# A two-layer decoder trunk in split fp32: layers written out, one weight slot merged, first low parts made on chip, one projection spread among the first logits

## The reference

```python
for l in range(DEPTH):                       # DEPTH = 2, S = 512, D = 1024, D_FF = 2816
    x = x + 0.5 * swiglu(rms_norm(x, ffn1_norm[l]), ffn1_gate[l], ffn1_up[l], ffn1_down[l])
    h = rms_norm(x, mix_norm[l])
    z = h @ w_in[l]
    aq, ak, av, iq, ik, iw, pu, mq = jnp.split(z, IN_OFFSETS, axis=-1)
    # aq, ak: 8 heads x 64, rms-normed; iq: 4 x 64; ik: 64; iw: 4; pu: 4 x 64; mq: 4 x 64
    y_attn = dsa_attention(aq, ak, av, iq, ik, iw)
    y_pool = multiscale_pool(pu, w_pool[l], pool_scale[l])
    y_mem = memory_attention(mq, rms_norm(mem, mem_norm[l]), w_mem_kv[l], ...)
    x = x + jnp.concatenate([y_attn, y_pool, y_mem], axis=-1) @ w_out[l]
    x = x + 0.5 * swiglu(rms_norm(x, ffn2_norm[l]), ffn2_gate[l], ffn2_up[l], ffn2_down[l])
```

## Time and profile before

| | us |
|---|---|
| median of 3 runs | 1970.55 |
| lowest, highest | 1969.13, 1972.46 |
| the profiled execution, its own time | 1967.57 |
| its span | 1965.5 |
| TensorE busy in it | 1918.9 |
| VectorE, ScalarE, GpSimd busy | 614.1, 1082.7, 347.6 |

### The profile page before, as it was taken

One profiled execution on the slowest core, in us unless ns is written; L12 is line 12 of the kernel. 1 busy time (PEld: TensorE's weight loads), 2 busy tenths in 40 slices (PEclk: granted clock), 3 DMA queues, 4 the chain that ended last, 5 costly groups with the idle time before them and its releaser, 6 DMA issues.

```text
span 1965.5 us, 27449 instructions
## 1 busy us (share of the span) xinstructions
PE 1918.9 (98%) x9148; PEld 1559.4 (79%) x9148; DVE 614.1 (31%) x1176; ACT 1082.7 (55%) x1391; POOL 347.6 (18%) x400
## 2 busy tenths in 40 slices
PE   6999999999899999999999999999998999999999
PEld 4888888887668888888878888888876688888887
DVE  3222210367662322220052222004677542222101
ACT  6655543565475755553375556336656566565432
POOL 1111111112511111111111111111125011111110
PEclk9999999999999999999999999999999999999999
DMA  8988888788236888888868888888781279888887
GB/s 219 215 190 191 194 193 193 184 197 193 76 87 150 199 197 191 192 193 192 194 162 201 191 193 189 199 192 199 177 205 48 70 173 221 192 193 193 194 190 184
DMA packets 97703, 354.07 MB, mean 180 GB/s; under 512 B 10976, under 2 KB 11232, under 8 KB 97376
## 3 DMA queue, kind: packets, MB, share of 16 engines
q0 software_dynamic: 47232, 171.99, 49.2%
q1 hardware_dynamic: 49824, 178.81, 27.7%
q10 hardware_dynamic: 576, 2.36, 0.3%
HBM read 179.05 MB, written 2.10 MB: 92 GB/s over the span
## 4 chain that ended last, share of the span: by engine, by line
PE 94%; DMA 2%; DVE 1%; issue 1%; ACT 1%; DVEq 0%; SPq 0%; ACTq 0%; POOLq 0%
PE bank L472 92%; PE bank L821 1%; DMA w_lo<-raw 1%; DMA raw<-weights 1%; ACT w_lo L932 0%; DMA x<-x_t 0%; DVE z L1315 0%; DVE mk_n L1321 0%; ACT prob L1086 0%; DVE t L1364 0%; ACT kv L1049 0%; ACT t L1086 0%; ACT w_hi L931 0%; DVE pt L344 0%; PE bank L744 0%
## 5 line engine op out<-in xcount | busy, mean ns | idle before, releaser
L931 ACT ACTIVATE w_hi<-raw 128x1024 fp32r<-128x1024 f32 x329 | 348.4, 1059 | 617.6 <-PE bank L472 592.1
L472 PE MATMUL bank<-h_hi,w_hi 128*128 128x512 f32 x1664 | 656.0, 394 | 15.6 <-ACT h_hi L903 13.6
L472 PE MATMUL bank<-h_hi,w_lo 128*128 128x512 f32 x1664 | 651.5, 392 | 5.7 <-DMA w_lo<-raw 5.7
L472 PE MATMUL bank<-h_lo,w_hi 128*128 128x512 f32 x1664 | 634.3, 390 | 0.0
L395 POOL DMA_DIRECT2D w_lo<-raw x328 | 282.6, 863 | 1556.5 <-ACT w_lo L932 1517.3
L472 PEld LDWEIGHTS bank<-h_hi,w_hi 128*128 128x128 f32 x1664 | 314.9, 189 | 88.5 <-ACT h_hi L903 15.1
L472 PEld LDWEIGHTS bank<-h_hi,w_lo 128*128 128x128 f32 x1664 | 314.7, 189 | 71.9 <-DMA w_lo<-raw 6.2
L472 PEld LDWEIGHTS bank<-h_lo,w_hi 128*128 128x128 f32 x1664 | 313.2, 188 | 66.2 <-issue 1.4
L932 ACT ACTIVATE w_lo<-raw 128x1024 fp32r<-128x1024 f32 x329 | 342.8, 1042 | 0.0
L472 PE MATMUL bank<-a_hi,w_hi 128*128 (+1 forms) x832 | 324.6, 390 | 0.0
L472 PE MATMUL bank<-a_lo,w_hi 128*128 (+1 forms) x832 | 323.8, 389 | 0.0
(11 more groups left out here) (143 smaller groups left out, 1226.2 us busy)
## 6 DMA issues: line engine op xcount, KB each, us to landing
raw<-weights SPq DMA_DIRECT2D x332, 512.0 KB, 4.7
w_lo<-raw POOLq DMA_DIRECT2D x328, 512.0 KB, 5.8
x<-x_t SPq DMA_DIRECT2D x4, 512.0 KB, 7.1
mem<-mem_t ACTq DMA_DIRECT2D x2, 1024.0 KB, 7.4
out_t<-x SPq DMA_DIRECT2D x8, 256.0 KB, 2.2
const<-consts SPq DMA_DIRECT2D x1, 481.5 KB, 10.0
wpool<-pool_w ACTq DMA_DIRECT2D x2, 128.0 KB, 7.2
par<-params SPq DMA_DIRECT2D x1, 38.0 KB, 1.8
```

The lines of the kernel that those rows point to most:

```text
L472: return nc.tensor.matmul(out_, lhsT, rhs, start=start, stop=stop, skip_group_check=True)
L931: nc.scalar.activation(w_hi[:, s], raw[:, s], ACT.Copy).then_inc(w_hi_done, 1)
```

## The change

- The two layers are written out on every engine instead of looped; the ring place of a slot is now `(l * SLOTS + n) % RING` (`place_of`), and the four dummy slots at the end of the stream are gone.
- ik and iw share one slot (64 columns and 4 columns); VectorE copies ik to both halves of `idx` in two operations. A layer has one slot fewer.
- In the indexer's section VectorE's work is reordered: the squares of the memory come after `cols`, the eight low parts of the memory (`m_lo`) after the scores; ScalarE rounds ik's successor after `idx_hi`.
- At the start SyncE issues slot 0 first. ScalarE writes its high part; VectorE writes its low part by subtraction, and both parts of slot 1; GpSimd both parts of slot 2. GpSimd also passes on that x has landed.
- At the start of the second layer `project_first` takes the order of the other thirds, and ScalarE rounds ahead at the end of the first layer as elsewhere.
- ScalarE loads the table with Silu before each ffn loop.
- In the tail mq 1 goes ahead of the spread, pu 0 and `heads_sum(2)` ahead of the transposes of `mk_n`. pu 1 goes in three pieces behind the logits of units 0, 2 and 4 (`RAMP`), into bank 5; VectorE evacuates it at unit 6. The first `pool_map` moves from unit 28 to 30.

```diff
-MIX_SLOTS = (("iq", 2), ("ik", 1), ("iw", 1), ("av", 4), ("aq", 4), ("ak", 4), ("kv", 4), ("mq", 2),
+MIX_SLOTS = (("iq", 2), ("ik", 1), ("av", 4), ("aq", 4), ("ak", 4), ("kv", 4), ("mq", 2),
...
-POOL_UNITS = (28, 32)
+POOL_UNITS = (30, 32)
+RAMP = {0: (4, 5, 6), 2: (7, 0, 1), 4: (2, 3)}
...
+            load(0, 0)
+            sp.dma_start(par[:, :], params[:, :]).then_inc(params_loaded, 16)
+            load_x(0)
+            load_x(1)
+            load(1, 1)
+            load_x(2)
+            load_x(3)
+            load(2, 2)
...
+                if pos < BEGUN:
+                    sp.wait_ge(first_lo[pos], 1)
...
+            pool.wait_ge(w_loaded[2], 16)
+            G.tensor_copy(w_hi[:, s], raw[:, s]).then_inc(first_hi[1], 1)
+            pool.wait_ge(first_hi[1], 1)
+            G.tensor_tensor(out=w_lo[:, s], in0=raw[:, s], in1=w_hi[:, s].bitcast(f32),
+                            op=ALU.subtract).then_inc(first_lo[2], 1)
...
-                if ph == 0:
-
-                    pe.wait_ge(w_hi_done, l * SLOTS + (n + 1))
+                if l == 0 and ph == 0:
+
+                    pe.wait_ge(w_hi_done, 1)
...
-                project(l, at("iw"), bank[3][:, :], h_hi, h_lo)
...
+                project_z(13, "mq", 1)
+
                 pe.wait_ge(spread_ready, l + 1)
...
-                project_z(13, "mq", 1)
-
-
+                project_z(14, "pu", 0)
+                heads_sum(2)
                 pe.wait_ge(mk_n_ready, l + 1)
...
-                project_z(14, "pu", 0)
-                heads_sum(2)
-                project_z(15, "pu", 1)
                 root_columns(2)
...
-                pe.wait_ge(proj_ready, (l + 1) * PROJ)
+                pe.wait_ge(proj_ready, (l + 1) * PROJ - 1)
...
+                    if n in RAMP:
+                        pool_part(RAMP[n])
...
-            with pe.Fori(0, LAYERS) as l:
+            for l in range(LAYERS):
...
+                nc.scalar.preload_act_table(ACT.Silu)
...
-                for n in range(rounds * RING, FC - 1 if e == 0 else FC - RING + 1):
+                for n in range(rounds * RING, FC - RING if l == LAYERS - 1 and e == 1 else FC - 1):
...
+                    if n == 6:
+                        evacuate(15, MIX_BASE["pu"] + 1, chunk(u, 1), bank[5][:, :], r[:, :])
...
+            V.tensor_tensor(out=w_lo[:, 0:SLOT], in0=raw[:, 0:SLOT], in1=w_hi[:, 0:SLOT].bitcast(f32),
+                            op=ALU.subtract).then_inc(first_lo[0], 1)
+            s = slice(SLOT, 2 * SLOT)
+            dve.wait_ge(w_loaded[1], 16)
+            V.tensor_copy(w_hi[:, s], raw[:, s]).then_inc(first_hi[0], 1)
...
```

More of the change, by code:

```diff
@@ L80 @@
 X_PARTS = 4
+BEGUN = RING - 1
 NEG = -1e30
@@ L321, in query_tile, with place_of, lo_count @@
         return TT - 1 - g // 2
+    def place_of(l, n):
+        return (l * SLOTS + n) % RING
+    def lo_count(l, n):
+        at = l * SLOTS + n
+        return 16 * (at // RING + (0 if at % RING < BEGUN else 1))
     passed = sem("passed")
@@ L455, in _ @@
                 pooling(l)
-                first = -(-(ahead + RING) // RING) * RING
-                for n in range(ahead, first):
-                    rest(l, (0, n))
-                with pool.Fori(0, (SLOTS - first) // RING) as i:
-                    for pos in range(RING):
-                        rest(l, (i * RING, first + pos))
-            assert steps[0] == POOL_CHAIN, steps[0]
+                rests(l, ahead, SLOTS if l == LAYERS - 1 else SLOTS + BEGUN)
+                assert steps[0] == POOL_CHAIN, steps[0]
         @block.tensor
@@ L491, in with_hi @@
                 def with_hi(i, k, part):
-                    mm(bank[i][:, :], weight((n + i) % RING, k * P)[part], chunk(h_hi, k),
+                    mm(bank[i][:, :], weight(place_of(l, n + i), k * P)[part], chunk(h_hi, k),
                        part == 0 and k == 0, False)
@@ L1121, in mix @@
                     round_ahead(l, MIX_BASE["out"] + k)
+            nc.scalar.preload_act_table(ACT.Silu)
+            act.wait_ge(w_loaded[0], 16)
+            nc.scalar.activation(w_hi[:, 0:SLOT], raw[:, 0:SLOT], ACT.Copy).then_inc(w_hi_done, 1)
             act.wait_ge(params_loaded, 16)
-            round_ahead(0, -RING)
-            with act.Fori(0, LAYERS) as l:
+            for l in range(LAYERS):
                 ffn(l, 0)
```

174 lines of the change are left out of this document (97 added, 77 removed).

## The result

| us | before | changed |
|---|---|---|
| median | 1970.03 (1969.13 to 1972.46, 4 runs) | 1943.5 (1942.63 to 1946.54, 4 runs) |
| span of the profiled execution | 1965.5 | 1940.8 |

What follows compares the result with a forecast made beforehand. TensorE, busy for 1918.9 of 1965.5 us, was taken as the bound. The terms -7.0 - 10.9 - 5.4 - 3.8 - 2.7 = -29.8 took 1967.57 to 1937.8 us profiled, 1940.8 for the median, range 1931 to 1951.

Steps and rivals of the forecast that it cites:

- 1, the start: Program start: TensorE's first sum of squares comes earlier, partly delayed by GpSimd disturbing VectorE; -7.0 us, range -4 to -10.4.
- 2, one slot fewer: Mix of both layers: the iw projection's 24 matmuls are gone, 5.44 us each; -10.9 us, range -5.4 to -10.9.
- Rival (c): Mix: the iw slot was partly cover, VectorE sets the pace, half the slot's gain is hidden; -24.4, 1946.2 us, chance 0.07.
- 3, between the layers: Start of the second layer: new TensorE order and slots rounded ahead; -5.4 us, range -4.5 to -5.5.
- 4, the tail: Mix's tail and first logits: reordered mq 1, pu 0 and pu 1 save 1.9 us a layer, -3.8 in all.
- rival (b): The tail gives nothing, half the `rt` wait moves on and the start is late; -21.7, 1948.9 us, chance 0.20.
- 5, the pool maps: First pool_map, moved two units later, no longer waits 1.4 us a layer for `rt`; -2.7 us, range 0 to -2.8.
- The later pooling: Mix: GpSimd's pooling starts some 8 us later after the first logits than before, and that stays hidden.
- Edits at nothing: Silu table load ahead of the loops and dropped dummy slots: no gain; vanished register instructions: a few tenths in the tail.
- Rival (d): Mix: the low clock stays through the logits after the added 4.7 us wait; slower, +40, 2011 us, chance 0.02.

Runs made afterwards that it cites:

- experiment 1: Changed kernel, but GpSimd begins on weight slot 2 only after VectorE's three sums of the squares; 1943.82 us, ratio 0.987.
- 5: Changed kernel, but at the start ScalarE and a DMA split weight slot 2, without GpSimd's two operations; 1940.54 us, ratio 0.9852.
- experiment 4: Changed kernel with iw in a weight slot of its own again, 24 more matmuls in each layer; 1957.51 us, ratio 0.9946.
- 7: Changed kernel, but between the layers TensorE takes the old order again, weights still rounded ahead; 1944.24 us, ratio 0.9866.
- 10: Changed kernel, but between the layers both TensorE's order and ScalarE's rounding are as before the change; 1949.74 us, ratio 0.9899.
- 3: Changed kernel with pu 1's eight pieces in TensorE's idle stretches: six ahead of `heads_sum(2)`, two ahead of the roots' transposes; 1937.41 us, ratio 0.9845.
- run 2: Changed kernel with the tail of the mix as it was before the change; 1943.55 us, ratio 0.9868.
- 8: Changed kernel without the Silu table load ahead of the ffn loops; 1945.38 us, ratio 0.9885.
- 9: Changed kernel with TensorE's first sum behind slot 2's fourth step, pu 1's pieces placed six, one, one, and first logits waiting for less; 1933.11 us, ratio 0.9814.
- 11: Changed kernel with the tail of experiment 9, the first sum behind slot 2's third step, and slot 4's rounding ahead of the root; 1928.88 us, ratio 0.9799.
- 12: Changed kernel with the rearranged tail of experiment 9 alone, start as changed; 1932.25 us, ratio 0.9818.
- 6: Changed kernel with three edits: slot 2 split by ScalarE and a DMA, pu 1's pieces five, one, one, one, `cols` matmuls spread out; 1935.44 us, ratio 0.9824.

## Why the prediction was right, and where it wasn't

**1, the start: right, the disturbance a little too large.** -8.26 against -7.0. The sum came at 24.35 here, and at 23.7 to 25.3 in the seven other profiles with the same start; it moves with the landing of x. The prediction had the sum at 22.2 undisturbed, and it came at 22.58 and 21.59 in experiments 1 and 5. It added 3.4 of the full exclusion's 5 us for GpSimd; it measured 2.95 on the low parts (experiment 1), 2.5 of them at the sum. That TensorE's own work ends at about 22 was right too (18.23 + 4.19).

**2, one slot fewer: right.** 5.44 us a layer (68.02 to 62.58, experiment 4). Rival (c), the slot as cover, is out: no new wait for VectorE appeared. The pair of traces shows 1.3 less than 10.9 in all, because of the low clock behind the tiny matmuls in layer 0, which the prediction didn't have.

**3, between the layers: right in size, not in its parts.** -5.42, and 10.88 us from the first matmul with `h_hi` to the sum, as forecast. The prediction put it on the order and the rounding ahead together; with the slots rounded ahead the order gives nothing (7), the rounding gives 4.1 (10), and the other 1.4 fit the table load (1.28 us) that is gone with the loop.

**4, the tail: the step that failed.** Forecast -1.9 a layer, measured -2.58 and +0.93, and next to nothing on the mean of many layers (51.0 against 51.1): rival (b)'s "the tail gives nothing". Cut in two at the first logits, the means of the same layers show where it went:

| mean of layers, us | old tail (4) | new tail (14) | difference | forecast |
|---|---|---|---|---|
| `heads_sum(1)` to the first logits | 38.9 | 34.0 | -4.9 | -6.0 |
| first logits to those of unit 6 | 6.1 | 10.9 | +4.8 | +2.3 + 1.85 |

The -6.0 was read off layer 0 and came true there (-6.08, wait 4.44 for 4.7). But the 1.53 us wait for `kv`, which mq 1 was to fill, stands in layer 0 alone: in layer 1 the first logits had come at 38.98, not 39.63. From there to unit 6 the prediction had 8.4 us at the full clock. It takes 9.7 (four layers of the fourteen), and 10.7 to 12.2 in the ten others, where matmuls run at the low level. The term that was mis-sized is a group of logits among pieces. I had 0.68 from its start to the next one's; it is 0.9, the first projection matmul behind it takes 0.34 instead of 0.23, and a group with three pieces comes to 3.2 where I had 2.7. The pieces didn't have to be so dear; they stood in the wrong place (3), beside 4.4 us of idle time that the change itself had made.

In layer 1 another 1 us went into a DMA. The chain of waits there has:

```profile
1434.36 10.17 DMA w_lo<-raw
```

It is the low part of mq 1, which came 0.81 us late for TensorE; the change takes mq 1 one spread earlier. In four others of the fourteen layers the spread of the key norms was 0.3 to 0.8 us late, in three of them with a wait for a low part ahead of it.

**5, the pool maps: the wait went, half of the gain with it.** -0.73 a layer on the stretch from the fourth to the fifth spread (11.47 to 10.74), where -1.35 was forecast. What is late next is VectorE's copy of `pt`:

```profile
546.84 0.41 PE L863 MATMUL bank<-const,t 128*128 128x128 f32 x2 [0.79 <-DVE pt L358]
...
547.76 1.12 PE L507 MATMUL bank<-u,wpool 128*128 128x512 f32 x2
```

And the stretch from the first to the last spread gained nothing at all (+0.05, +0.20): its first three intervals are 0.5 to 0.6 longer, the last three 0.2 and 0.4. With the old tail (2) and the early pieces (3) the first ones are 0.3 to 0.4 shorter again. The later pooling isn't the reason: it ends 8 us behind the first spread before and in run 2, and 16 to 17 us behind it both in the changed kernel and in run 3. TensorE waits for `pt` in these intervals and nowhere for the pooling, so that part of the prediction holds. What delays `pt` was not tried.

**Edits at nothing: right** for the Silu load (8); the loop over the layers hid one table load, as said under 3. Rival (d) didn't come: the longest stretch at the low level in the changed kernel, waits included, is that from 1461.19 to 1469.97, about 9 us, and some 10 in experiment 7; the pace then came back among the first logits. The errors of the five terms are -1.3, +1.3, 0, +2.2 and +2.9, so the profiled execution gained 24.7 and not 29.8. That the median is only 2.7 us over the forecast is in part luck: the profiled execution is 4.8 over its own (1942.63 for 1937.8), and 2 us come back because I had carried over 2.98 us between profiled run and median where the changed kernel has 0.9.

## What to carry to other kernels

Reorder a stretch and the bound moves: fill the wait that the new order opens with the work you were going to spread elsewhere, then read which engine has no idle row left, and only then relax what its consumers wait for. Here that took the tail from 51 to 44.6 us a layer (experiments 9, 11 and 12) where the reordering alone gave nothing. Price such a stretch in each layer by itself: a wait that one layer has, another may lack. An engine's queue that waits for a late result holds back everything behind it (ScalarE's for 6.8 us in experiment 9), so put what is not dependent (a rounding for the next slot) ahead of the wait. TensorE has 98% of the span here: the slot taken out paid in full, 5.44 us a layer, and moved work paid only where it filled idle time.

## What the runs showed of the hardware

- **The clock falls from 2.4 to 1.2 GHz at short waits too, and not always.** Behind a wait of 1.9 us of TensorE at the start the stretch from the first sum to the mix's sum took 360.0 us in four profiles and 361.6 in four others with the same start; behind the 1.8 us waits of experiments 5 and 6 no matmul ran at the low level. Three waits of 1.3, 1.1 and 1.0 us among small matmuls brought the low level back in both layers of experiment 3; before, waits of 0.4, 1.1 and 1.1 us in the same place didn't. Sixteen tiny matmuls in a row, with next to no idle time, did it in 9 of 22 layers. Each costs 1.0 to 2.5 us. Of the 5.8 us between the profiles of the changed kernel and of experiment 7 the low clock makes all (1.6 at the start, 1.6 behind the tiny matmuls, 2.5 and 0.2 at the first logits); a later start (+0.9) and a low part that was late in one alone (-0.8) cancel. Effects of 2 us have to be read from the stretch that they touch.
- **GpSimd and VectorE on SBUF slow each other down**: 0.75 to 1.53 and 2.90 us for VectorE's low parts of 128x512, 1.03 to 1.41 and 2.33 to 2.73 for GpSimd's cast and subtraction of 128x1024. Without the overlap (experiments 1 and 5) all eight low parts took 0.74 or 0.75.
